# A second multiplication, by one, in GpSimd's scaling of probability tiles (two-layer diffusion backbone, one core)

## The chip, the cores and the metric

The kernel runs on one core of one Trainium2 chip. The metric is the device time of the whole program in microseconds (us), lower is better. Engines are named as the profile names them: PE is TensorE (matmul; PEld its weight loads), DVE is VectorE, ACT is ScalarE, POOL is GpSimd, SP is SyncE, which only issues DMAs here. All arithmetic is fp32, or fp32 split in a high and a low part for the matmuls.

## The reference

Two layers of a diffusion backbone work on 512 latent and 256 context tokens of width 1024. Each layer is a gated feed-forward block, a mixer, and another feed-forward block. The mixer has three branches: a window attention with a sink (A), a global attention (B) and a Fourier mix (C). The part that the change touches is the softmax of A and B:

```
s = jnp.einsum('bqkgd,bskd->bkgqs', q, k) * scale        # A: band of +-128 keys, plus context keys, plus a sink logit
p = jax.nn.softmax(jnp.concatenate([s_lat, s_ctx], -1), axis=-1)
o = jnp.einsum('bkgqs,bskd->bqkgd', p, v)
```

Both branches have 6 query heads that share 2 key/value heads (so 3 query heads, g = 0, 1, 2, to one key/value head). Context queries see context keys alone. In the second layer the context is not updated, so only latent queries are computed there.

## The kernel before

**The attention stage.** The work is cut in score tiles of 128 queries of one head. A tile (b, kv, q, g) is branch b, key/value head kv, query block q, query head g; the list is ordered by b, then kv, q and g. Three consecutive tiles (g = 0, 1, 2) share q and are called a triple here. There are 72 tiles in the first layer (q = 0 to 5; 4 and 5 are context) and 48 in the second (q = 0 to 3). A tile of branch B with latent queries has 768 keys; one of branch A has 512 keys at the ends of the sequence and 640 between; a context tile has 256.

One tile i goes through these steps, each engine in its own program order:

1. PE: scores(i) into the PSUM tensor ring[i % 2] (L1782 to L1790).
2. DVE: neg_max (L1272), the negated row maximum.
3. ACT: exp into the SBUF tile prob[i % 4], with row sums (L1151).
4. DVE: row_inv, the reciprocal of the row sum (L1280).
5. The scaling prob = prob * row_inv. For g = 0 it is done by DVE itself (L1285), for g = 1 and 2 by POOL (L753), which waits for the semaphore inv_ready.
6. PE: transposes the scaled tile in 128-column blocks into PSUM row (L1807); it waits for scaled_dve or scaled_pool.
7. ACT: the high part pth (L1127); DVE: the low part ptl (L1297).
8. PE: the product with the values for a whole triple (L1823); ACT and DVE add its two halves (acc L1140, rstd L1314; the latter buffer holds osum there).
9. POOL: split_out, which rounds the triple's output to xh (L740) and puts the rest in xl (L744).

**What sets the order.** Everything is written out by hand, with semaphores. PE issues in turn i: scores(i), the transposes of tile i - 3 (LAG = 3), and a third of the value products of an earlier triple. prob has 4 buffers (P_RING), freed when PE has transposed the tile (p_turned). POOL's queue in this stage holds only the two scalings of each triple and, from tile 11 on, one split_out behind each triple's second scaling. The g = 2 scaling of a triple is thus followed by two short instructions before the next triple's g = 1 scaling. POOL issues no DMA.

The other stages of the kernel are feed-forward blocks and the projections into and out of the mixer. There POOL adds weight tiles (L642 to L656) and sums of squares (L705, L708).

Of the kernel before, what the change touches and what calls it, by code (L numbers as in the profile page):

```python
# [18 lines left out]
ALU = mybir.AluOpType  # L19
# [7 lines left out]
TOK = SEQ + CTX  # L27
# [23 lines left out]
P_RING, LAG = 4, 3  # L51


def w_in_width(layer, j):

    return TOK if layer < DEPTH - 1 or j in (VA, VB, KA, KB) else SEQ
# [7 lines left out]
def halves(width):  # L64

    return [(0, SEQ, 0, 0), (SEQ, TOK, SEQ, 1)] if width == TOK else [(0, SEQ // 2, 0, 0), (SEQ // 2, SEQ, SEQ, 0)]
# [139 lines left out]
def key_blocks(branch, q):  # L206

    if q >= 4:
        return []
    return list(range(max(0, q - 1), min(3, q + 1) + 1)) if branch == 0 else [0, 1, 2, 3]  # L210


def build(nc, x_t, ctx_t, c_cols, c_rows, w_first, w_turned, b_ada, gains, g_final, qk_gain, sink, w_in, w_four, w_out,
# [4 lines left out]
    with ctx:  # L218
        sem_of = {}

        def sem(name):
            sem_of[name] = ctx.enter_context(nc.semaphore(name))
            return sem_of[name]
# [5 lines left out]
        def sb(name, shape, dt=F32, offset=None):  # L229
            size = int(np.prod(shape[1:])) * (2 if dt == BF16 else 4)  # L230
            if offset is None:
                offset = at[0]
                at[0] += size + 31 & ~31
            return nc.alloc_sbuf_tensor_at(name, shape, dt, offset=offset)
# [27 lines left out]
        row_inv = sb("row_inv", [P, 8])  # L262
# [58 lines left out]
        prob = sb("prob", [P, P_RING, TOK], F32, work + 43008)  # L321
# [54 lines left out]
        scaled_dve, scaled_pool = sem("scaled_dve"), sem("scaled_pool")  # L376
# [57 lines left out]
        def square_count(s, d, p):  # L434


            return s["squares"] + d + 1 + (KD - s["whole"] if p == 1 and d >= s["whole"] else 0)

        def sum_count(s, d, p):


            return s["sums"] + d + 1 + (KD - 1 - s["whole"] if p == 1 and d >= s["whole"] else 0)
# [231 lines left out]
        @block.gpsimd  # L674
        def _(pool):
            pool.memset(ones[:], 1.0).then_inc(consts_ready, 1)
            pool.memset(head_sel[:], 0.0).then_inc(consts_ready, 1)
            pool.memset(ident[:], 0.0).then_inc(consts_ready, 1)
            pool.memset(ident_b[:], 0.0).then_inc(consts_ready, 1)
            pool.memset(band_mask[:], 0.0).then_inc(consts_ready, 1)  # L680
            pool.memset(eps[:], NORM_EPS).then_inc(consts_ready, 1)
            pool.wait_ge(consts_ready, 6)
            pool.memset(head_sel[0:HD, 0:1], 1.0).then_inc(consts_ready, 1)
            pool.wait_ge(consts_ready, 7)
            pool.memset(head_sel[HD:P, 1:2], 1.0).then_inc(consts_ready, 1)
            pool.wait_ge(consts_ready, 8)
            for m in (ident, ident_b):
                pool.affine_select(out=m[:], in_=m[:], compare_op=ALU.not_equal, fill=1.0, base=0,
                                   pattern=[[-1, P]], channel_multiplier=1).then_inc(consts_ready, 1)

            pool.affine_select(out=band_mask[:, 0], in_=band_mask[:, 0], compare_op=ALU.is_ge, fill=NEG_INF,
                               base=0, pattern=[[1, P]], channel_multiplier=-1)
            pool.affine_select(out=band_mask[:, 1], in_=band_mask[:, 1], compare_op=ALU.is_ge, fill=NEG_INF,
                               base=0, pattern=[[-1, P]], channel_multiplier=1).then_inc(consts_ready, 1)

            def sum_squares(s):

                width, whole = s["out_width"], s["whole"]
                steps = [(d, 0, (0, width)) for d in range(whole)]
                steps += [(d, p, halves(width)[p][0:2]) for p in range(2) for d in range(whole, KD - 1)]  # L700
                for d, p, (a, b) in steps:
                    pool.wait_ge(sq_done, square_count(s, d, p))
                    if d == 0:
                        pool.wait_ge(ssq_ready, 2 * (s["n"] + 1))
                        pool.tensor_copy(acc[:, a:b], sq[:, 0, a:b]).then_inc(acc_done, 1)  # L705
                    else:
                        pool.wait_ge(acc_done, sum_count(s, d, p) - 1)
                        pool.tensor_tensor(acc[:, a:b], acc[:, a:b], sq[:, d % 2, a:b], ALU.add).then_inc(acc_done, 1)  # L708

            pool.wait_ge(sq_first[1], 2)  # L710
            pool.tensor_tensor(acc[:, SEQ:TOK], sq_ctx[:, 0], sq_ctx[:, 1], ALU.add).then_inc(acc_first[1], 1)
            for d in range(2, KD - 1):
                pool.wait_ge(sq_first[1], d + 1)
                pool.wait_ge(acc_first[1], d - 1)
                pool.tensor_tensor(acc[:, SEQ:TOK], acc[:, SEQ:TOK], sq_ctx[:, d], ALU.add).then_inc(acc_first[1], 1)
            for s in stages:
                layer, n, ow = s["layer"], s["n"], s["out_width"]
                if s["kind"] == "mix":
                    pool.wait_ge(x_ready, X_STEPS * (n + 1))
                    pool.memset(wf[:], 0.0).then_inc(wf_zeroed, 1)  # L720
                    pool.wait_ge(tab_loaded, 16 * (layer + 1))
                    for q in range(8):
                        g, sl, width = 8 * layer + q, q % 2, w_in_width(layer, q)
                        pool.wait_ge(rot_done, g + 1)
                        if q >= 2:
                            pool.wait_ge(qlo_done, g - 1)
                        if width == TOK:
                            pool.tensor_copy(roped[:, sl, SEQ:TOK], un[q % 3][:, SEQ:TOK])
                        pool.tensor_tensor(rot[:, sl], rot[:, sl], rope_tab[:, 1], ALU.mult).then_inc(rope_done, 1)
                        pool.wait_ge(rope_done, 2 * g + 1)  # L730
                        pool.tensor_tensor(roped[:, sl, 0:SEQ], rot[:, sl], ucos[:, sl], ALU.add).then_inc(rope_done, 1)
                    def split_out(k, issued):

                        pool.wait_ge(scaled_pool, (s["scores"] + issued) // 3 * 2 + max(0, issued % 3 - 1))
                        b, kv, q, g = s["tiles"][3 * k]
                        tr = s["scores"] // 3 + k
                        here, cols = slice(kv * HD, kv * HD + HD), slice(q * P, (q + 1) * P)
                        pool.wait_ge(osum_done, tr + 1)
                        o = osum[here, k % 2].rearrange("p (g q) -> p g q", q=P)
                        pool.tensor_copy(xh[here, 3 * b:3 * b + 3, cols], o).then_inc(ohi_done, 1)  # L740
                        pool.wait_ge(ohi_done, tr + 1)
                        if k >= 1:
                            pool.wait_ge(olo_done, tr)
                        pool.tensor_tensor(xl[here, 3 * b:3 * b + 3, cols], o,  # L744
                                           xh[here, 3 * b:3 * b + 3, cols].bitcast(F32), ALU.subtract).then_inc(olo_done, 1)

                    for i, (b, kv, q, g) in enumerate(s["tiles"]):
                        if g == 0:
                            continue
                        si = s["scores"] + i  # L750
                        lo = SEQ - P * len(key_blocks(b, q))
                        pool.wait_ge(inv_ready, si + 1)
                        pool.tensor_scalar(prob[:, i % P_RING, lo:TOK], prob[:, i % P_RING, lo:TOK], row_inv[:, i % 8:i % 8 + 1], None,  # L753
                                           ALU.mult).then_inc(scaled_pool, 1)
                        if g == 2 and i >= 11:
                            split_out(i // 3 - 3, i + 1)
                            pool.wait_ge(olo_done, s["scores"] // 3 + i // 3 - 2)
                    for k in range(len(s["tiles"]) // 3 - 3, len(s["tiles"]) // 3):
                        split_out(k, len(s["tiles"]))
                    pool.wait_ge(olo_done, (s["scores"] + len(s["tiles"])) // 3)  # L760
                    sum_squares(s)
                    continue
                pool_ffn(pool, s, sum_squares)
# [1442 lines left out]
```

## Time and profile before

| what | value |
|---|---|
| time, median of 3 runs | 2590.87 us (2587.87 to 2591.29) |
| span of the profiled execution, first to last instruction | 2588.9 us |
| mean granted PE clock over the span | 0.994 |
| attention stage of the first layer | about 700 to 840 us |
| attention stage of the second layer | about 2060 to 2165 us |
| POOL busy in L753 in these two stretches | 77.87 and 61.84 us |

The span is the only time of the profiled execution itself. The median of the runs is 2.0 us above it; they are the whole program's times, with what lies ahead of the first instruction and behind the last. Busy times are of one profiled execution. An engine can be near 100% busy in one stage and idle in another, so the table names the stages that the change lies in.

### The profile page before, as it was taken

The numbers are of one execution on the slowest core, as the hardware profiler recorded it, in microseconds if no ns is written. First come the engines' busy times: TensorE is split into PE (matmuls) and PEld (weight loads), VectorE is DVE, ScalarE is ACT, GpSimd is POOL, SyncE is SP. The second block draws the span as 40 slices with busy tenths as digits, with TensorE's granted clock in tenths as the row PEclk, the third lists the DMA queues.
The fourth block names the chain that finished last, engine by engine and source line by source line (L and its number), as shares of the span: only waits on it lengthen the run. The fifth ranks groups of instructions, "written<-read, shape, count | busy, mean of one in ns | idle before, by whom it ended". The sixth has DMA issues, their size and how long they took to land.

```text
span 2588.9 us, 40436 instructions
## 1 busy us (share of the span) xinstructions
PE 2509.8 (97%) x14986; PEld 2309.4 (89%) x14986; DVE 1942.3 (75%) x3285; ACT 1156.9 (45%) x2203; POOL 790.3 (31%) x614
## 2 busy tenths in 40 slices
PE   7999999999988999999999999999999999999998
PEld 4999999988887899999999899999998788899997
DVE  5788788766498588888755888887557596877776
ACT  4533433443377362433344624333444485544444
POOL 1322221224188231222122312221222285333332
PEclk8999999999999999999999999999999999999999
DMA  6344444214430124444312244443123431133332
GB/s 243 103 143 143 128 135 147 84 53 146 122 91 1 58 86 134 131 139 147 114 57 74 86 135 131 139 147 114 58 70 110 124 78 50 62 95 102 106 100 79
DMA packets 132002, 276.17 MB, mean 107 GB/s; under 512 B 15584, under 2 KB 35296, under 8 KB 130528
## 3 DMA queue, kind: packets, MB, share of 16 engines
q1 hardware_dynamic: 131808, 273.60, 34.7%
q8 instruction: 120, 1.97, 0.3%
q14 instruction: 74, 0.61, 0.1%
HBM read 260.43 MB, written 13.11 MB: 106 GB/s over the span
## 4 chain that ended last, share of the span: by engine, by line
PE 80%; DVE 13%; issue 3%; ACT 2%; POOL 1%; DMA 1%; SPq 0%; DVEq 0%; ACTq 0%; POOLq 0%
PE ring L1887 36%; PE ring L1992 23%; PE ring L2003 15%; DVE wlo L1482 3%; DVE neg_max L1272 2%; DVE ptl L1297 1%; PE row L1823 1%; PE ring L1843 1%; PE row L1807 1%; DVE xl L1593 1%; DVE prob L1285 1%; DVE rstd L1314 1%; DMA ada_early<-w_turned 1%; DVE t_lat L1586 0%; POOL prob L753 0%
## 5 line engine op out<-in xcount | busy, mean ns | idle before, releaser
L1482 DVE TENSOR_TENSOR wlo<-raw,whi 128x512 fp32r<-128x512 f32 (+2 forms) x672 | 506.5, 764 | 297.1 <-ACT whi L973 295.9
L973 ACT ACTIVATE whi<-raw 128x512 fp32r<-128x512 f32 (+2 forms) x672 | 399.2, 605 | 373.5 <-PE ring L1992 231.5
L1887 PE MATMUL ring<-xh,whi 128*128 128x384 f32 (+1 forms) x1280 | 413.2, 323 | 10.4 <-DVE rstd L1461 5.7
L1887 PE MATMUL ring<-xl,whi 128*128 128x384 f32 (+1 forms) x1280 | 411.4, 321 | 0.0
L1887 PE MATMUL ring<-xh,wlo 128*128 128x384 f32 (+1 forms) x1280 | 411.2, 321 | 0.0
L656 POOL TENSOR_TENSOR raw<-raw,s_two 128x512 f32<-128x512 f32 x80 | 122.9, 1536 | 628.8 <-DVE wlo L1482 587.2
L1887 PE MATMUL ring<-th,whi 128*128 128x384 f32 (+1 forms) x960 | 311.8, 325 | 2.9 <-DVE wlo L1482 2.0
L1887 PE MATMUL ring<-th,wlo 128*128 128x384 f32 (+1 forms) x960 | 310.8, 324 | 0.0
L1887 PE MATMUL ring<-tl,whi 128*128 128x384 f32 (+1 forms) x960 | 310.7, 324 | 0.0
L1489 DVE SCALAR_TENSOR_TENSOR ada_junk<-ada_tile,row 128x1024 bf16<-128x1024 f32 x256 | 301.4, 1214 | 0.0
L642 POOL TENSOR_TENSOR s_one<-raw 128x512 f32<-128x512 f32 x80 | 105.6, 1321 | 550.8 <-DMA raw<-w_gu 413.0
L1887 PEld LDWEIGHTS ring<-xh,whi 128*128 128x128 f32 x1280 | 241.0, 188 | 14.7 <-DVE rstd L1461 8.1
L1887 PEld LDWEIGHTS ring<-xl,whi 128*128 128x128 f32 x1280 | 241.1, 188 | 0.7
L1887 PEld LDWEIGHTS ring<-xh,wlo 128*128 128x128 f32 x1280 | 241.2, 188 | 0.0
L1602 DVE SCALAR_TENSOR_TENSOR h<-ring,vec_gate,h 128x512 f32<-128x512 f32 x250 | 149.2, 631 | 86.4 <-PE ring L1992 52.9
L1992 PE MATMUL ring<-act_hi,wlo 128*128 128x512 f32 (+1 forms) x714 | 196.9, 345 | 0.0
L1992 PE MATMUL ring<-act_hi,whi 128*128 128x512 f32 (+1 forms) x714 | 196.6, 345 | 0.0
L1992 PE MATMUL ring<-act_lo,whi 128*128 128x256 f32 (+1 forms) x714 | 196.6, 345 | 0.0
L1887 PEld LDWEIGHTS ring<-th,whi 128*128 128x128 f32 x960 | 180.5, 188 | 4.2 <-issue 2.0
L1887 PEld LDWEIGHTS ring<-tl,whi 128*128 128x128 f32 x960 | 180.5, 188 | 0.0
L1887 PEld LDWEIGHTS ring<-th,wlo 128*128 128x128 f32 x960 | 180.3, 188 | 0.0
L753 POOL TENSOR_SCALAR prob<-prob,row_inv 128x768 f32<-128x768 f32 (+3 forms) x80 | 140.8, 1762 | 122.1 <-DVE row_inv L1280 120.7
(218 smaller groups left out, 5488.5 us busy)
## 6 DMA issues: line engine op xcount, KB each, us to landing
raw<-w_gu SPq DMA_DIRECT2D x352, 256.0 KB, 3.2
ada_tile<-w_turned SPq DMA_DIRECT2D x130, 512.0 KB, 3.7
raw<-w_down SPq DMA_DIRECT2D x96, 256.0 KB, 3.7
raw<-w_down SPq DMA_DIRECT2D x64, 192.0 KB, 2.5
raw<-w_in SPq DMA_DIRECT2D x48, 256.0 KB, 3.5
raw<-w_down SPq DMA_DIRECT2D x64, 128.0 KB, 2.1
raw<-w_out SPq DMA_DIRECT2D x32, 256.0 KB, 8.1
ada_first<-w_first SPq DMA_DIRECT2D x4, 1536.0 KB, 13.4
```

Of the source, the lines that this page charges most:

```text
L642: pool.tensor_tensor(s_one[:], raw[:, a21 % RAWS], raw[:, a22 % RAWS], ALU.add).then_inc(s_done, 1)
L656: pool.tensor_tensor(raw[:, a11 % RAWS], raw[:, a12 % RAWS], s_two[:], ALU.subtract).then_inc(s_done, 1)
L753: pool.tensor_scalar(prob[:, i % P_RING, lo:TOK], prob[:, i % P_RING, lo:TOK], row_inv[:, i % 8:i % 8 + 1], None, ALU.mult).then_inc(scale ...
L973: act.activation(weights(q, 0, cols)[0], src[:, 0:cols], ACT.Copy).then_inc(whi_ready, 1)
L1272: dve.reduce_max(neg_max[:, i % 4:i % 4 + 1], ring[i % 2][:, lo:TOK], AX.X, negate=True).then_inc(nm_ready, 1)
L1285: dve.tensor_scalar(prob[:, j % P_RING, lo:TOK], prob[:, j % P_RING, lo:TOK], row_inv[:, j % 8:j % 8 + 1], None, ALU.mult).then_inc(scaled ...
L1482: dve.tensor_tensor(w_l, src[:, 0:cols], w_h.bitcast(F32), ALU.subtract).then_inc(wlo_ready, 1)
L1489: dve.scalar_tensor_tensor(out=junk[:, c], in0=tile, scalar=1.0, in1=rows[:, c], op0=ALU.mult, op1=ALU.mult, accum_out=modv[:, c, i:i + 1] ...
L1602: last = dve.scalar_tensor_tensor(out=h[:, d, a:b], in0=ring[slot][:, a:b], scalar=vec_gate[:, c, d:d + 1], in1=h[:, d, a:b], op0=ALU.mult ...
L1887: last = pe.matmul(out, w, x, start=(start and k == 0 and m == 0), stop=(k == HALF - 1 and m == 2), skip_group_check=not start)
L1992: last = pe.matmul(out[:, a:b], w, x[:, k, a:b], start=(k == 0 and m == 0), stop=(k == parts[-1][1] - 1 and m == 2))
L2003: last = pe.matmul(out[:, o:o + b - a], w, x[:, k, a:b], start=(k == 0 and m == 0), stop=(k == parts[-1][1] - 1 and m == 2))
```

## The change

The scaling on POOL was a tensor_scalar instruction with one operation, a multiplication by the per-row reciprocal. It becomes a tensor_scalar with two operations: a multiplication by the same reciprocal and then one by the constant 1.0. The values are the same. It is still one instruction per tile, on the same tiles, in the same place, with the same wait and the same semaphore update. The number and order of instructions on each engine stay as they are. DVE's own scaling of the g = 0 tiles (L1285) keeps its one operation.

```diff
                         pool.wait_ge(inv_ready, si + 1)
-                        pool.tensor_scalar(prob[:, i % P_RING, lo:TOK], prob[:, i % P_RING, lo:TOK], row_inv[:, i % 8:i % 8 + 1], None,
-                                           ALU.mult).then_inc(scaled_pool, 1)
+                        pool.tensor_scalar(prob[:, i % P_RING, lo:TOK], prob[:, i % P_RING, lo:TOK], row_inv[:, i % 8:i % 8 + 1], 1.0,
+                                           ALU.mult, ALU.mult).then_inc(scaled_pool, 1)
```

## Rows read from the trace of the kernel before

**Rows 1.** The page, busy time by engine, share of the span, instructions.
```profile
PE 2509.8 (97%) x14986; PEld 2309.4 (89%) x14986; DVE 1942.3 (75%) x3285; ACT 1156.9 (45%) x2203; POOL 790.3 (31%) x614
```
**Rows 2.** Busy time in stretches: length, PE, PEld, DVE, ACT, POOL, clock, DMA, GB/s.
```profile
700.00:830.00 130.00, 113.74 (x783) 100.90 (x783) 121.99 (x279) 103.75 (x259) 105.92 (x83) 1.00 0.19 46
2064.00:2156.00 92.00, 85.92 (x596) 78.03 (x595) 89.94 (x189) 75.60 (x174) 76.26 (x53) 1.00 0.23 55
```
**Rows 3.** The instructions of L753: min/median/max ns, forms; waits (us, times).
```profile
L753 POOL TENSOR_SCALAR prob<-prob,row_inv x80: 922/1886/2542, 700.1 to 2157.7; 128x768 f32<-128x768 f32 x32, 128x512 f32<-128x512 f32 x16, 128x640 f32<-128x640 f32 x16, 128x256 f32<-128x256 f32 x16
...
  DVE row_inv L1280: 120.7, 48
...
  PEld row L1807: 4.1, 8
  PE row L1807: 2.5, 7
```
**Rows 4.** POOL by line and shape: count, busy us, mean ns, idle before.
```profile
L753 POOL TENSOR_SCALAR prob<-prob,row_inv 128x768 f32<-128x768 f32 x32 | 70.9, 2219 | 10.4 <-DVE row_inv L1280 10.0
...
L753 POOL TENSOR_SCALAR prob<-prob,row_inv 128x256 f32<-128x256 f32 x16 | 14.8, 923 | 7.9 <-DVE row_inv L1280 7.2
```
**Rows 5.** The same view, other POOL instructions of two sizes each.
```profile
L708 POOL TENSOR_TENSOR acc<-acc,sq 128x256 f32<-128x256 f32 x34 | 29.5, 868 | 77.4 <-ACT sq L979 77.2
...
L708 POOL TENSOR_TENSOR acc<-acc,sq 128x768 f32<-128x768 f32 x6 | 11.1, 1847 | 24.4 <-ACT sq L979 24.4
...
L705 POOL COPY acc<-sq 128x768 f32<-128x768 f32 x4 | 3.3, 826 | 96.8 <-ACT sq L979 87.9 <-issue 8.9
L705 POOL COPY acc<-sq 128x512 f32<-128x512 f32 x2 | 1.2, 611 | 21.4 <-ACT sq L979 16.4 <-issue 4.9
```
**Rows 6.** The chain that ended last, POOL's pieces in it: start, length (us).
```profile
785.09 1.67 POOL prob L753
...
787.27 2.21 POOL prob L753
...
801.38 1.60 POOL prob L753
...
803.57 2.55 POOL prob L753
...
822.08 2.05 POOL prob L753
...
824.26 2.22 POOL prob L753
```
**Rows 7.** PE in order of time: start, us, idle before it and releaser.
```profile
789.53 0.87 PE L1807 MATMUL row<-ident,prob 128*128 128x128 f32 x6 [0.32 <-POOL prob L753]
...
803.64 0.87 PE L1807 MATMUL row<-ident,prob 128*128 128x128 f32 x6 [0.39 <-POOL prob L753]
...
806.16 0.87 PE L1807 MATMUL row<-ident,prob 128*128 128x128 f32 x6 [0.60 <-POOL prob L753]
```
**Rows 8.** POOL in order of time, parts of a 640-key and a 768-key triple.
```profile
742.75 1.88 POOL L753 TENSOR_SCALAR prob<-prob,row_inv 128x640 f32<-128x640 f32 x1 [0.32 <-DVE row_inv L1280]
745.02 1.89 POOL L753 TENSOR_SCALAR prob<-prob,row_inv 128x640 f32<-128x640 f32 x1 [0.39 <-DVE row_inv L1280]
...
778.19 4.46 POOL L753 TENSOR_SCALAR prob<-prob,row_inv 128x768 f32<-128x768 f32 x2 [0.57 <-DVE row_inv L1280]
782.71 0.70 POOL L740 CAST xh<-rstd 64x384 fp32r<-64x384 f32 x1
783.50 1.01 POOL L744 TENSOR_TENSOR xl<-rstd,xh 64x384 fp32r<-64x384 f32 x1
785.09 4.39 POOL L753 TENSOR_SCALAR prob<-prob,row_inv 128x768 f32<-128x768 f32 x2 [0.57 <-DVE row_inv L1280]
```
**Rows 9.** DVE's own scalings, two of them, in order of time.
```profile
782.28 0.77 DVE L1285 TENSOR_SCALAR prob<-prob,row_inv 128x768 f32<-128x768 f32 x1
...
804.82 0.62 DVE L1285 TENSOR_SCALAR prob<-prob,row_inv 128x768 f32<-128x768 f32 x1
```

## The prediction

> **What bounds the kernel now.** I read the page's busy times first. PE is busy 97% of the span and POOL 31% [rows 1], so over the whole kernel POOL is no bound. But every edited instruction lies in the two attention stages, so I read those stretches alone [rows 2]. There the picture turns: DVE is busy 121.99 of 130 us in the first layer and 89.94 of 92 in the second (94% and 98%), PE 87% and 93%, POOL 81% and 83%. DVE sets the pace and POOL is not far behind. Third, I asked who waits at the edited line. POOL waits for DVE's reciprocal 120.7 us in 48 waits, most of it ahead of each stage; PE waits for POOL only 2.5 us in 7 waits, and its weight loads 4.1 us in 8 [rows 3]. Last, the chain that ended last shows where POOL is the late one nonetheless: in six instructions, all in the global branch of the first layer, around 785, 801 and 822 us, 12.3 us together [rows 6]. These are the places where a run of 768-key tiles borders on the short context tiles, and DVE and POOL run out of step. In the second layer no piece of the chain is a POOL scaling.
>
> **What a scaling costs now.** 2219 ns for 768 columns and 923 ns for 256 [rows 4], so (2219 - 923) / 512 = 2.53 ns per column and 923 - 256 x 2.53 = 275 ns fixed. Two neighbours [rows 5]: a copy takes (826 - 611) / 256 = 0.84 ns per column; an addition of two tensors takes (1847 - 868) / 512 = 1.91. So the one-operation tensor_scalar, with one tensor input, is slower per column than an instruction that reads two tensors and also does one operation. Its time is thus neither the input nor the single arithmetic operation; it is the way in which this form is executed.
>
> **The change, part by part.** Nothing is removed or moved: 80 instructions (32 of 768 columns, 16 each of 640, 512 and 256 [rows 3]) get another form. The only term is the length of that form, which the trace doesn't show. Bounds for a 768-column tile:
> - Fast end: it streams like the copy, 275 + 768 x 0.84 = 920 ns, 1.30 us less.
> - Middle: like the two-tensor addition, 275 + 768 x 1.91 = 1742 ns, 0.48 us less.
> - No change: 2219 ns, if both stages of the instruction are always executed.
> - Slow: the second operation costs one more column step of 0.84 ns, +0.65 us; or as much again as the first adds to a copy (2.53 - 0.84 = 1.69 ns), +1.30 us.
>
> I take the faster side, with no firm value between 920 and 1742 ns: the two rows of other two-port or one-port streams both lie under the present rate, so the present form is the odd one out, and a form with both operations given need not go through the same code. That is a choice, not a reading.
>
> The Trainium skill (GPSIMD Engine Reference, 3.1 Elementwise: side-by-side cycle accounting) says that a body with at most two operations per element is bound by the ports at 1.03 cycles per element, at a clock of 1.2 GHz. By that both forms would take about 0.86 ns per column. The trace speaks against it for the one-operation form (2.53 ns, three such cycles); for the form with two no row here shows it.
>
> **What a shorter scaling is worth.** Where DVE is saturated, nothing: POOL already waits for DVE ahead of a triple (0.57 us idle [rows 8]) and would only wait longer. It is worth something where PE waits for POOL. That is 2.5 us in PE's own waits [rows 3], for instance 0.32, 0.39 and 0.60 us [rows 7]. The chain holds more, 12.3 us in six pieces; at the fast end these would shrink by 6 x 1.30 = 7.8 us if nothing else were late. But something is: at 789.53 PE came to the transposes only 0.32 us before POOL was done, so behind POOL's 2.21 us piece PE's own queue is late by 1.9 us. I therefore take PE's waits, -2.5 us, and keep -7.8 us as the end. The middle length, 0.48 us less, covers most of these waits as well (each is at most 0.6 us in the rows shown), so the value hardly depends on which length it is. All of DVE's idle time in the two stretches is 8.0 + 2.1 = 10.1 us [rows 2], which caps any gain.
>
> Sum for the profiled execution: 2588.9 - 2.5 = 2586.4 us. The median of the runs stands 2.0 us above that span, so 2590.9 - 2.5 = 2588.4 us.
>
> **Rivals.**
>
> *A, the length doesn't change* (both stages are always executed). Then nothing changes at all: 2590.9 us. For it: one instruction, one read and one write stream as before. Against it: nothing in the trace.
>
> *B, the second operation is paid for, and POOL becomes the bound of the attention stage.* A 768-key triple repeats every 785.09 - 778.19 = 6.90 us, with 0.57 us idle, about 0.1 of it the usual gap between instructions, so POOL's slack is about 0.47 us per triple, or 0.24 us per scaling [rows 8]. That is the point from which it decides. With +0.65 us per scaling the triple grows by 1.30 - 0.47 = 0.83 us; there are 32 / 2 = 16 such triples: +13 us. A 640-key triple has 0.71 us of waits, some 0.6 to spare, where split_out also runs (4 of the 8 triples); it needs 2 x 0.54 = 1.07: +0.5 x 4 = 2 us. The six pieces on the chain add some 2 to 4 us, since PE's queue takes part of them. Total about +18 us: 2609 us. With +1.30 us per scaling: 16 x (2.60 - 0.47) = 34, the 640-key triples 4 x 1.5 = 6, the 512-key ones some 4, and the places on the chain 3: +47 us, 2638 us. For it: one operation already costs 1.69 ns per column more than a copy, so operations are perhaps what is charged for. Against it: an addition of two tensors, also one operation, costs less.
>
> *C, the scaling gets short, but it now collides with DVE.* DVE's scaling of a 768-column tile took 0.62 us at 804.82, wholly beside a POOL scaling, and 0.77 us at 782.28, where a POOL cast followed, itself lengthened to 0.70 us [rows 9, 8]; the POOL scaling beside the first took 2.55 us in place of 2.2 [rows 6]. So the two slow each other a little. A POOL scaling that streams like a copy uses its memory port more densely. If each of DVE's 40 scalings lost 0.3 us, DVE, which is the bound, would add 12 us, less 2.5: about +9 us, 2600 us. Against it: the POOL scaling would also be in progress for less than half as long.
>
> The Trainium skill (SBUF: State Buffer, Who interferes with whom) says that a DVE instruction in a two-port mode and GpSimd hold a shared pair of ports as an exclusive lock, the other waiting for the whole instruction. Under it DVE's scaling at 804.82 would have waited until 806.12; it took 0.62 us, so this trace shows a small loss and no such block.
>
> **How the numbers follow.** Shorter scaling, gain of 1 to 4 us as a rule: 0.47, its own range 2585 to 2590. Rival A: 0.25. Rival B: 0.22, with both ends about as likely. Rival C: 0.06. The likeliest case gives 2588.4 us. 0.2% is 5.2 us, about what a measurement of this kernel can tell from no change. Faster by more than that needs a gain well beyond PE's waits, towards the 7.8 us: a little over a quarter of the first case, 0.13. Slower: nine tenths of B and half of C, 0.23. The same: the rest, 0.64. The range 2584 to 2611 leaves out the far gains (0.05) and the upper part of B (0.12).
>
> **What would show it right or wrong.** In the profile after, the 768-column rows of L753 should have a mean between 900 and 1800 ns, the idle time of POOL ahead of them should grow by what they lose, and DVE should stay at 94% and 98% of the two stretches or rise. PE's waits for POOL's prob should fall to nearly nothing and L753 should leave the chain. The three places at 785, 801 and 822 us should each close up by well under a microsecond to 1.5 us. A mean over 2.5 us for that row would make the forecast wrong, through rival B, and then the wait of POOL for row_inv should be gone and PE's wait for POOL should be tens of microseconds. DVE's L1285 rows growing from some 0.77 us would be rival C. An unchanged 2219 would be rival A.

## The result and the profile after

| kernel | median, us | runs |
|---|---|---|
| before | 2589.21 (2587.13 to 2591.29) | 11 |
| changed | 2595.03 (2592.32 to 2600.8) | 11 |

The ratio is 1.0023, with a 95% interval of 1.0015 to 1.0031: 5.8 us slower, small but clear of no change. The spans of the two profiled executions differ by 5.4 us: 2594.3 and 2588.9 us. The forecast had been 2.5 us faster. One execution of a later kernel, e9, took 4107.32 us at a granted clock of 0.555; it is left out of every ratio, and without it that kernel's median would be 2589.55 us in place of 2590.19.

The first view to read is POOL by line and shape (count, busy us, mean ns, idle before it), for the edited line in the changed kernel:

```profile
L753 POOL TENSOR_SCALAR prob<-prob,row_inv 128x768 f32<-128x768 f32 x32 | 29.1, 911 | 58.4 <-DVE row_inv L1280 58.4
...
L753 POOL TENSOR_SCALAR prob<-prob,row_inv 128x640 f32<-128x640 f32 x16 | 12.9, 803 | 30.5 <-DVE row_inv L1280 30.5
L753 POOL TENSOR_SCALAR prob<-prob,row_inv 128x512 f32<-128x512 f32 x16 | 11.1, 696 | 104.2 <-DVE row_inv L1280 104.2
...
L753 POOL TENSOR_SCALAR prob<-prob,row_inv 128x256 f32<-128x256 f32 x16 | 7.7, 482 | 17.5 <-DVE row_inv L1280 17.4
```

The instruction does twice the multiplications in less than half the time: 911 ns in place of 2219 [rows 4], 0.84 ns per column in place of 2.53, the rate of a copy [rows 5]. Over the 80 instructions, summed over the four shapes, that is 60.8 us of POOL's time in place of 140.8. Yet the kernel is slower. It is not that somebody now waits for POOL: in the changed kernel no engine waits for L753 any more, where PE had waited 2.5 us and its weight loads 4.1 us [rows 3]. The loss is on another engine. DVE's busy time by line, first the changed kernel and then the one before (no other DVE line of the attention stage moved by more than 0.2 us):

```profile
L1285 DVE TENSOR_SCALAR prob<-prob,row_inv 128x768 f32<-128x768 f32 (+3 forms) x40 | 36.0, 901 | 1.4
```
```profile
L1285 DVE TENSOR_SCALAR prob<-prob,row_inv 128x768 f32<-128x768 f32 (+3 forms) x40 | 26.7, 668 | 1.4
```

L1285 is DVE's own scaling of the g = 0 tiles, which the change doesn't touch. It takes 9.3 us more, at 768 columns 1194 ns in place of 770:

```profile
L1285 DVE TENSOR_SCALAR prob<-prob,row_inv 128x768 f32<-128x768 f32 x16 | 19.1, 1194 | 0.6
```

DVE bounds these stages [rows 2], so what it loses counts. What it loses the time to can be seen when POOL and DVE are put in order of time (start us, length us), here in the changed kernel. Compare this with [rows 8] and [rows 9]:

```profile
774.25 0.92 POOL L753 TENSOR_SCALAR prob<-prob,row_inv 128x768 f32<-128x768 f32 x1 [1.71 <-DVE row_inv L1280]
...
775.24 0.50 POOL L740 CAST xh<-rstd 64x384 fp32r<-64x384 f32 x1
775.83 1.01 POOL L744 TENSOR_TENSOR xl<-rstd,xh 64x384 fp32r<-64x384 f32 x1
776.04 1.21 DVE L1285 TENSOR_SCALAR prob<-prob,row_inv 128x768 f32<-128x768 f32 x1
```

POOL finishes the g = 2 scaling early, so the two instructions of split_out behind it, L740 and L744, run early too. L744 (two tensors read from SBUF) now starts at 775.83, just ahead of DVE's scaling at 776.04, and ends at 776.84. DVE's scaling ends at 777.25, 0.41 us later. All 16 scalings of 768 columns meet L744 in this way, and so do some shorter ones. L744 has 0.70 to 0.96 us left when the 16 begin, and each ends 0.41 to 0.43 us behind it. The lengths of the same instruction undisturbed (the first experiment below: 621 ns at 768 columns, 354 at 256) give 0.52 ns per column, or 0.40 us for 768. So its streaming took place wholly behind L744, and most of the time before was a wait inside the instruction. In the kernel before, POOL's long g = 2 scaling came ahead of this moment: one triple later, L744 came at 783.50, after DVE's scaling at 782.28 was over.

The Trainium skill (SBUF: State Buffer, Who interferes with whom) describes this: a DVE instruction in a two-port mode and GpSimd share a pair of ports as an exclusive lock, and whichever is issued second is blocked until the other ends. For L744 the trace agrees, in both orders: behind it DVE's scaling waited as above, and where DVE was first by 0.06 us, DVE kept its 0.49 us and L744 took 1.29 in place of 1.01 us:

```profile
746.29 0.49 DVE L1285 TENSOR_SCALAR prob<-prob,row_inv 128x512 f32<-128x512 f32 x1
746.35 1.29 POOL L744 TENSOR_TENSOR xl<-rstd,xh 64x384 fp32r<-64x384 f32 x1
```

### The profile page after: what moved, and what is told of

It is laid out like the page before. It is cut to its first block, busy times and chain, and to the rows that moved or that the text cites. A ratio compares the mean times of both kernels' runs of the same rounds, so it can differ in the third digit from the quotient of the medians.

```text
span 2594.3 us, 40436 instructions
## 1 busy us (share of the span) xinstructions
PE 2510.0 (97%) x14986; PEld 2308.2 (89%) x14986; DVE 1953.7 (75%) x3285; ACT 1156.8 (45%) x2203; POOL 708.2 (27%) x614
## 4 chain that ended last, share of the span: by engine, by line
PE 80%; DVE 13%; issue 3%; ACT 2%; DMA 1%; SPq 0%; POOL 0%; DVEq 0%; ACTq 0%; POOLq 0%
PE ring L1887 36%; PE ring L1992 23%; PE ring L2003 15%; DVE wlo L1482 3%; DVE neg_max L1272 2%; DVE ptl L1297 2%; PE row L1823 1%; PE ring L1843 1%; PE row L1807 1%; DVE rstd L1314 1%; DVE prob L1285 1%; DMA h<-x_t 1%; DVE xl L1593 1%; DVE acc L1337 1%; DVE t_lat L1586 0%
## 5 line engine op out<-in xcount | busy, mean ns | idle before, releaser
L949 ACT ACTIVATE acc<-acc 128x768 f32<-128x768 f32 (+1 forms) x80 | 63.5, 793 | 173.2 <-DVE acc L1467 173.2
```

Source lines behind the costliest of these rows:

```text
L949: act.activation(c1[:, 0:width], c1[:, 0:width], ACT.Silu).then_inc(silu_done, 1)
```

## The experiments

The collision theory: a shorter g = 2 scaling lets L744 start just ahead of DVE's g = 0 scaling, which then waits inside itself. Rival 1: the new form slows DVE by its denser stream wherever split_out stands (the mechanism of case C in the prediction). Rival 2: the early end of POOL's work reorders PE's, and DVE's longer instruction is incidental.

### split_out moved off the collision (e1_split_g1)

```diff
-                        if g == 2 and i >= 11:
+                        if g == 1 and i >= 10:
                             split_out(i // 3 - 3, i + 1)
```

> The changed kernel, with POOL's split_out (L740 and L744) issued behind the g = 1 scaling of a triple in place of the g = 2 scaling. Collision theory (the loss is that DVE's g = 0 scaling, L1285, now meets POOL's two-input L744 and waits until it ends): L744 then runs while DVE does its row maximum and its low parts, so L1285 at 768 columns falls from 1194 ns to about 620 to 650, DVE loses 9 us of busy time, and the time is 2584 to 2588 us, below the kernel before. Rival 1 (the two-operation form itself slows DVE, by a denser stream, wherever split_out stands): L1285 stays near 1.1 to 1.2 us and the time near 2595. Rival 2 (the earlier end of POOL's work reorders PE's work, and L1285 is incidental): L1285 falls but the time stays near 2595.

Measured: 2585.37 us, ratio to the kernel before 0.998 (0.9971 to 0.9989). Rival 1 falls, since the form is that of the changed kernel and L1285 fell all the same. Rival 2 falls with the time. (The g = 2 scaling doesn't end quite as early here as in the changed kernel, as the rows below show; L744 cut short, further below, leaves its end alone and settles this.) DVE's 40 scalings fell by 14.9 us to 21.1, where 9 us had been expected. DVE's scaling in this kernel:

```profile
L1285 DVE TENSOR_SCALAR prob<-prob,row_inv 128x768 f32<-128x768 f32 x16 | 9.9, 621 | 0.6
```

All of the 16 now take 0.62 us. So 621 ns is what it costs alone, and the 770 ns of the kernel before already held a wait of 0.15 us each on average. POOL in order of time in this kernel, from the L744 of one triple on:

```profile
777.42 1.01 POOL L744 TENSOR_TENSOR xl<-rstd,xh 64x384 fp32r<-64x384 f32 x1
778.53 0.91 POOL L753 TENSOR_SCALAR prob<-prob,row_inv 128x768 f32<-128x768 f32 x1
```
and DVE's scaling behind it, in the same kernel:
```profile
780.03 0.62 DVE L1285 TENSOR_SCALAR prob<-prob,row_inv 128x768 f32<-128x768 f32 x1
```

L744 is over at 778.43, and the g = 2 scaling at 779.44. Its reciprocal was there at 778.08, so L744 holds this scaling up by some 0.35 us. In this whole kernel only one weight load waits for a scaling of POOL, for 0.2 us. DVE's scaling finds POOL idle at 780.03.

### Half of the change, either half (e2_two_op_g1, e3_two_op_g2)

```diff
+                        ops = (1.0, ALU.mult, ALU.mult) if g == 1 else (None, ALU.mult)     # e2; in e3 g == 2
-                        pool.tensor_scalar(prob..., row_inv..., 1.0, ALU.mult, ALU.mult)
+                        pool.tensor_scalar(prob..., row_inv..., *ops)
```

> Only the g = 1 scalings have two operations; the g = 2 ones have one again. Collision theory: the g = 2 scaling ends where it did, so split_out stands where it stood: L1285 at 768 columns near 770 ns and 2587 to 2590 us, as before or a little below. Rival 1 (the form itself slows DVE): half of the loss stays, about 2592 us, with L1285 near 980 ns.

> Only the g = 2 scalings have two operations. Collision theory: POOL is done with the one-operation g = 1 scaling before the g = 2 reciprocal comes, so split_out starts as early as with the full change: L1285 at 768 columns near 1190 ns and 2593 to 2596 us, the whole loss from half of the edit. Rival 1: half of the loss, about 2592 us, L1285 near 980 ns.

Measured: 2587.93 us with the g = 1 scalings shortened, ratio 0.9992 (0.9981 to 1.0002), and 2596.36 us with the g = 2 ones, ratio 1.0026 (1.0017 to 1.0035), 0.4 us above its expected range. The two halves shorten the same number of instructions by the same time, and one carries no loss, the other all of it. What tells them apart is only whether the instruction directly ahead of split_out ends early. DVE's scaling of 768 columns, first with g = 1, then with g = 2 shortened (in these two kernels the line is L1286):

```profile
L1286 DVE TENSOR_SCALAR prob<-prob,row_inv 128x768 f32<-128x768 f32 x16 | 12.3, 768 | 0.6
```
```profile
L1286 DVE TENSOR_SCALAR prob<-prob,row_inv 128x768 f32<-128x768 f32 x16 | 18.7, 1170 | 0.6
```

### The new place with the old form (e4_before_split_g1)

The same edit as in the first experiment, made to the kernel before.

> The kernel before (one operation) with split_out behind the g = 1 scaling. It tells whether the new place is good by itself. Collision theory: POOL's g = 2 scaling now starts some 1.3 us later and ends while or after DVE's g = 0 scaling runs; PE waits for POOL: 2590 to 2600 us, not faster than before. If the place by itself were the gain, it would be 2584 to 2588 us here too.

Measured: 2603.61 us, ratio 1.0057 (1.0045 to 1.007), 3.6 us above the upper end of what was expected. The place alone is bad: with scalings of 2.2 us, POOL's g = 2 scaling now ends late and PE waits for it, 18.8 us in 20 waits in place of 2.5 us in 7 (and its weight loads 22.8 us in 22 in place of 4.1 us in 8):

```profile
PE row L1807 <- POOL prob L753: 18.8, 20, 2.4
```

So of these two edits, the short form and the new place, each is a loss by itself and only both together are a gain.

### L744 cut to 3 of 384 columns (e5_thin_rest)

The changed kernel, in which L744 leaves out the low part of all but 3 columns of the attention output.

```diff
+                        one = slice(q * P, q * P + 1)
-                        pool.tensor_tensor(xl[here, 3 * b:3 * b + 3, cols], o, xh[here, 3 * b:3 * b + 3, cols]..., ALU.subtract)
+                        pool.tensor_tensor(xl[here, 3 * b:3 * b + 3, one], o[:, :, 0:1], xh[here, 3 * b:3 * b + 3, one]..., ALU.subtract)
```

> The changed kernel with L744 cut to 3 of its 384 columns (the low part xl of the attention output is left out for the rest, so the output differs); everything stays in its place. Collision theory: what DVE's g = 0 scaling waits for is L744 itself; with it shortened from 1.0 us to about 0.3 us, L1285 at 768 columns falls to 620 to 700 ns and the time to 2584 to 2588 us, as with split_out moved. Rival (DVE is slowed by the two-operation scalings or by the cast ahead of L744): L1285 stays above 1 us and the time near 2595.

Measured: 2584.27 us, ratio 0.9975 (0.9965 to 0.9985). L744 takes 214 ns here and DVE's scaling of 768 columns 621 ns, as with split_out moved, though everything stands where the change had put it. So L744 is what DVE waited for at 768 columns, and neither the early end of POOL's scalings nor the cast. The cast costs DVE little: one 256-column scaling that began 0.34 us before the end of the cast took 0.48 us in place of 0.35. The short scalings are not shown to be harmless, only out of the way: in this kernel none of them overlaps a DVE scaling.

### DVE's scaling moved instead of POOL's work (e9_dve_scale_late)

DVE issues the g = 0 scaling behind the two ptl instructions of its turn, in place of ahead of them.

> The changed kernel, POOL untouched; DVE issues its g = 0 scaling (L1285 before) behind the two low parts (ptl) of the same turn, about 1.0 us later. In the changed kernel L744 had 0.70 to 0.77 us left when that scaling came, in nearly all 768-key triples. Collision theory: the scaling now comes after the end of L744 and takes about 620 ns at 768 columns; 2584 to 2588 us. Rival (the loss sits on POOL's or PE's side): no better than 2595, or worse, since the g = 0 tile is ready for PE 0.4 us later.

Measured: 2590.19 us, ratio 0.9995 (0.9986 to 1.0005). The loss of the change is gone, but the further gain of the first experiment did not come, so the time missed its expected range by 2.2 us. In the run of 768-key tiles the scaling is at 0.61 us, and L1285's work over all 40 is 23.6 us, between the 26.7 of before and the 21.1 of the first experiment. Nine scalings still wait for L744, among the short tiles and at the start of each run of 768-key tiles. The rest of the miss looks like DVE's ptl instructions, which now wait for ACT 18 times for 8.6 us in the first layer's stage, against 9 times for 5.9 us with split_out moved. That this is the price of the new order was not tested by itself.

### All scalings on POOL (e6_all_pool, e7_all_pool_one_op, e8_all_pool_split_g1)

The g = 0 scaling is taken out of DVE's program, and POOL skips no tile; the counts of the semaphores follow. e6 has the two-operation form, e7 the one-operation form, e8 is e6 with split_out behind g = 1.

```diff
-            return (scaled_dve, k + 1) if g == 0 else (scaled_pool, 2 * k + g)
+            return scaled_pool, si + 1
...
-                    if g == 0:
-                        dve.wait_ge(inv_ready, sj + 1)
-                        dve.tensor_scalar(prob..., row_inv..., None, ALU.mult).then_inc(scaled_dve, 1)
...
-                        if g == 0:
-                            continue
```

> The changed kernel with the g = 0 scalings on POOL too, in two-operation form; DVE scales nothing. Collision theory: POOL needs 3 x 0.91 + 1.6 = 4.3 of some 6.5 us per 768-key triple, DVE is freed of all its port conflicts and of 27 us of work (9 more than that against the changed kernel); then PE (93% busy in the second layer's stretch, 87% in the first's) bounds: 2569 to 2578 us. If DVE was not what bound the stage, the time would stay at 2584 to 2589.

> The same with the one-operation form. POOL needs 3 x 2.22 + 1.6 + gaps = 8.6 us per 768-key triple in place of the 6.9 at which DVE ran, 16 times, and 7.6 in place of 5.9 in the 640-key ones: POOL bounds the stage, some 35 us slower, 2615 to 2635 us. It prices the form of the instruction: with e6 the difference should be 40 to 60 us.

> All scalings on POOL in two-operation form, and split_out behind the g = 1 scaling. DVE has no instruction left in the attention stage that could collide, so by the collision theory the place of split_out no longer matters: 2577 to 2582 us, the same as with split_out behind g = 2. If the place were good for another reason (an earlier end of the output split), it would be 3 us or more faster than that.

Measured:

| kernel | median, us | ratio to before (95%) |
|---|---|---|
| e6, two operations | 2579.5 | 0.9953 (0.994 to 0.9967) |
| e7, one operation | 2620.86 | 1.0116 (1.0102 to 1.0129) |
| e8, as e6, split_out behind g = 1 | 2579.44 | 0.9969 (0.9958 to 0.9981) |

e6 and e8 are the fastest kernels of the study, e6 8.5 to 15.5 us ahead of the one before by its interval; e8 can't be told from it, as the collision theory wants: with DVE's scalings gone, the place of L744 no longer matters. The median of e6 lies 1.5 us above its expected range; why PE stays a few per cent short of full there was not followed up. It is the form of the instruction that makes this split possible: the same kernel with one operation is 41 us slower. Stretches of e6 (length; busy PE, PEld, DVE, ACT, POOL; clock; DMA) against [rows 2]:

```profile
700.00:830.00 130.00, 118.22 (x822) 106.30 (x823) 114.61 (x268) 106.13 (x268) 81.29 (x113) 1.00 0.19 46
2064.00:2156.00 92.00, 87.50 (x596) 80.44 (x597) 80.78 (x169) 73.27 (x169) 56.30 (x70) 1.00 0.23 55
```

DVE has fallen from 94% and 98% to 88% in both, and PE has risen from 87% and 93% to 91% and 95%. PE is now the busier of the two. With one operation, POOL is the bound. In e7's first stretch it is 94% busy:

```profile
700.00:830.00 130.00, 107.33 (x703) 96.56 (x701) 100.37 (x227) 91.51 (x229) 121.99 (x94) 0.95 0.19 46
```

The granted clock is 0.95 there, in place of 1.00, and what that adds was not separated. It isn't what makes e7 slow: from 2100 to 2180 us, in the second layer's stage, the clock is 1.00 and POOL is still busy 77.48 of 80 us, PE 64.06.

### The runs side by side

DVE's busy time in its g = 0 scalings beside the time. The ratios are each to the kernel before as measured with that kernel, and are safer to compare than the medians, which come from different sets of runs:

| kernel | DVE's 40 scalings, us | median, us | ratio |
|---|---|---|---|
| e1, split_out behind g = 1 | 21.1 | 2585.37 | 0.998 |
| e5, L744 cut short | 21.2 | 2584.27 | 0.9975 |
| e9, DVE's scaling later | 23.6 | 2590.19 | 0.9995 |
| e2, two operations for g = 1 | 25.9 | 2587.93 | 0.9992 |
| e4, old form, split_out behind g = 1 | 26.6 | 2603.61 | 1.0057 |
| before | 26.7 | 2589.21 | 1 |
| changed | 36.0 | 2595.03 | 1.0023 |
| e3, two operations for g = 2 | 36.3 | 2596.36 | 1.0026 |

From e1 to the changed kernel DVE has 14.9 us more, and the time is 9.7 us longer by the medians and 11 us by the ratios. So two thirds to three quarters of what DVE loses is lost to the kernel. e4 falls out of the order, because PE waits for POOL there; e9 stands a little above its place in it; its section has what is known of that.

## Why the prediction was wrong

**What bounds the kernel: right.** DVE sets the pace of the attention stages, and the whole result hangs on it. Freed of its scalings, in e6, the kernel gains 10.7 us by the medians.

**What a scaling costs now, and the bounds: right.** The fast end, 920 ns at 768 columns, met 911. The prediction had called its faster side a choice and not a reading, and the choice came out: the one-operation form was the odd one out. The Trainium skill's 1.03 cycles per element (GPSIMD Engine Reference, 3.1 Elementwise: side-by-side cycle accounting), which the trace of before had contradicted for one operation, fits the form with two (0.84 ns per column, one cycle of 1.2 GHz).

**"Where DVE is saturated, nothing": this step failed.** The failed term is this "nothing". The prediction counted only what POOL's end releases on PE, and found 2.5 us of waits to be removed. They were removed, and L753 left the chain, as it had said. But its sum had no term for DVE, and DVE lost 9.3 us. It did not ask what stands behind the scaling in POOL's queue and where that moves to. split_out follows the g = 2 scaling; [rows 8] show it at 782.71 and 783.50, and 1.3 us earlier is on top of DVE's scaling, at 782.28 in [rows 9]. All of the rows for that arithmetic were there. A faster instruction moves the start of everything behind it on its engine, and here the next one but one is an instruction that the bound engine waits for.

The measured 2595.03 us lies inside the range of 2584 to 2611, but that is luck: the part of the range above 2590.9 stood for rival B, a longer scaling, and, with little weight, for C.

**Case C had the right victim and the wrong mechanism.** It expected DVE's scalings to grow through the denser stream of POOL's new form, 0.3 us each, 12 us in all, less 2.5, 2600 us; it gave that 0.06. They grew by 9.3 us in all, 0.23 us each on average, and the net loss was 5.8 us. But no two-operation scaling overlaps one of these DVE scalings in the changed kernel's two stages, and in e1 only three do, in their last 0.16 us or less, at no loss. What a dense stream would cost DVE was thus never tested; the cause was L744, moved in time.

**The reading behind the low chance was a mistake.** The prediction set aside the Trainium skill's rule of an exclusive lock (SBUF: State Buffer, Who interferes with whom) on one row: DVE's scaling at 804.82, 0.62 us beside a POOL scaling. It read the 0.77 us at 782.28 as slight friction with the cast that followed. That scaling in fact ended at 783.05, which is 0.40 us after POOL's scaling had ended (778.19 + 4.46 = 782.65). The one at 767.90 is the same:

```profile
764.08 4.39 POOL L753 TENSOR_SCALAR prob<-prob,row_inv 128x768 f32<-128x768 f32 x2 [0.57 <-DVE row_inv L1280]
...
767.90 0.98 DVE L1285 TENSOR_SCALAR prob<-prob,row_inv 128x768 f32<-128x768 f32 x1
...
768.53 0.70 POOL L740 CAST xh<-rstd 64x384 fp32r<-64x384 f32 x1
```

It ended at 768.88; POOL's scaling had ended at 768.47, 0.41 us before, and the cast, 0.70 in place of 0.50 us, was then itself held up. These were blocks, of 0.15 to 0.36 us, in the kernel before, and twelve of its 16 scalings of 768 columns show one, each ending 0.40 to 0.43 us behind POOL's scaling. Of the 13 that began inside a 768-column scaling of POOL only the one at 804.82 got through; the last section says why. Reading every pair of overlapping instructions, not one, would have shown the blocks and put much more weight on a collision.

**Rivals A and B** did not come: the length changed, and not upward. B's prices were not tested; e4 and e7 show only that a late POOL is dear in this kernel, with a loss of 0.57% (14.8 us by the medians) and of 1.16% (31 us).

## What to carry to other kernels

When an instruction gets shorter, follow its engine's queue past it: list what is issued next, how much earlier it starts, and what the bound engine is doing at that moment. An instruction whose length varies from 0.60 to 1.37 us at one shape, as DVE's scaling did over these kernels, is waiting inside itself, and comparing its end with the ends of the other engine's instructions shows for whom. A faster engine pays when the split of the work or the order is set anew for it: against the kernel before, the edit alone made it 5.8 us slower, with one neighbour moved as well 3 to 7 us faster, and with all scalings given to POOL 8.5 to 15.5 us faster.

## What the runs showed of the hardware

- GpSimd's tensor_scalar on fp32 with one multiplication takes 2.53 ns per column of 128 partitions, with two multiplications 0.84 (911 and 482 ns at 768 and 256 columns). A second operation that does nothing makes it 2.4 times as fast at 768 columns.
- DVE's fp32 tensor_scalar from SBUF to SBUF takes 621 ns at 768 columns alone and 354 at 256. Begun while GpSimd's two-input L744 runs, it ends 0.41 to 0.43 us behind that one's end at 768 columns, about the time that it needs to stream; begun before, it holds that one up (L744 1.29 in place of 1.01 us).
- GpSimd's one-operation scaling of 768 columns (2.20 us) holds DVE's up at its start and at its end, but not in between. In e4 DVE's scalings of 768 columns begin at many points of it. Those that began 0.19 to 0.65 us after POOL's took 1.11 to 0.66 us and all ended 1.30 or 1.31 us after POOL's start, as the first pair below. Those that began 0.71 to 0.89 us after it took their 0.62 us, and POOL's its 2.20. Begun 1.00 and 1.19 us after, DVE's still took 0.62, but POOL's grew to 2.29 and 2.48 us (second pair); the scaling at 804.82 of the kernel before, 1.25 us after, is of this kind. Begun 1.64 us after or later, DVE's waited for POOL's end. An estimate from these rows: 1.31 less 0.41 us of streaming gives 0.90 us for the end of the first hold, and DVE's end less what POOL lost (1.62 - 0.09, 1.81 - 0.28, 1.87 - 0.34) gives 1.53 us for the start of the second.

```profile
787.49 2.20 POOL L753 TENSOR_SCALAR prob<-prob,row_inv 128x768 f32<-128x768 f32 x1
787.69 1.11 DVE L1285 TENSOR_SCALAR prob<-prob,row_inv 128x768 f32<-128x768 f32 x1
...
2126.67 2.48 POOL L753 TENSOR_SCALAR prob<-prob,row_inv 128x768 f32<-128x768 f32 x1
2127.86 0.62 DVE L1285 TENSOR_SCALAR prob<-prob,row_inv 128x768 f32<-128x768 f32 x1
```

So this instruction does not hold DVE up over its whole length, and the scaling at 804.82 fell into the gap. The first hold is about as long as a whole two-operation scaling (911 ns); whether the one-operation form makes two passes over the tile is open. Open too is whether a two-operation scaling holds DVE up.
